# First modulation and first projections of a two-block transformer layer, worked tile by tile, on one Trainium2 core

## The reference, cut to what matters

```python
def first_block(x, c, w_in, b_gates, ..., w_ada, b_ada, ...):
    c_act = jax.nn.silu(c)
    h = layer_norm(x)
    for l in range(DEPTH):
        ada = (c_act @ w_ada[l] + b_ada[l])[:, None, :]
        sh1, sc1, g1, sh2, sc2, g2 = jnp.split(ada, 6, axis=-1)
        u = h * (1.0 + sc1) + sh1
        y = mixer(u, w_in[l], ...)      # z = u @ w_in; q/k, v, gates, attention
        ...
```

## Time and profile before

| | us |
|---|---|
| median of 3 runs | 1974.08 (1972.8 to 1978.43) |
| the profiled execution, its own time | 1963.49 |
| its span in the profile | 1961.7 |
| TensorE busy | 1897.7 |
| VectorE busy | 1419.5 |
| ScalarE busy | 1038.9 |
| mean granted clock of TensorE | 0.991 |

### The profile page before, as it was taken

The page is one execution under the profiler, slowest core; times in us unless marked ns, Lnnn a source line. Parts: engine busy times, 40 slices in busy tenths (PEclk is TensorE's granted clock), DMA queues, the critical chain, the costliest instruction groups (busy, mean ns, idle before and its releaser), DMA issues.

```text
span 1961.7 us, 37250 instructions
## 1 busy us (share of the span) xinstructions
PE 1897.7 (97%) x15702; PEld 1814.0 (92%) x15702; DVE 1419.5 (72%) x2563; ACT 1038.9 (53%) x1601; POOL 23.1 (1%) x36
## 2 busy tenths in 40 slices
PE   6999999999999999999999999999999999999998
PEld 5999999999999999999999988889999988799998
DVE  7887686687668876776675558996766589967665
ACT  3564465454446654664544434565655445666554
POOL 1100000000002000000000000000000000000000
PEclk7999999999999999999999999999999999999999
DMA  8555545548763565545465525332555443335552
GB/s 323 203 179 210 216 174 190 183 180 306 258 237 129 181 213 204 194 176 194 170 253 194 206 104 189 132 126 88 202 194 194 141 154 136 110 107 182 194 194 98
DMA packets 52770, 358.98 MB, mean 183 GB/s; under 512 B 5995, under 2 KB 8651, under 8 KB 9980
## 3 DMA queue, kind: packets, MB, share of 16 engines
q1 hardware_dynamic: 52476, 356.54, 50.8%
q10 hardware_dynamic: 128, 0.07, 0.0%
HBM read 355.41 MB, written 1.08 MB: 182 GB/s over the span
## 4 chain that ended last, share of the span: by engine, by line
PE 81%; DVE 12%; ACT 4%; issue 2%; DMA 2%; SPq 0%; ACTq 0%; DVEq 0%
PE projected L483 35%; PE projected L1534 18%; PE mixed L483 7%; PE mixed L1534 6%; PE projected L1552 2%; DVE W L2141 2%; DVE w_lo L400 2%; DVE w_lo L1476 1%; PE mixed L641 1%; PE projected L1588 1%; DMA w_mod<-in_first_ada_dram 1%; PE mixed L1686 1%; PE mixed L1659 1%; PE mixed L549 1%; PE mixed L562 1%
## 5 line engine op out<-in xcount | busy, mean ns | idle before, releaser
L400 DVE TENSOR_TENSOR w_lo<-raw,w_hi 128x1024 fp32r<-128x1024 f32 x340 | 409.2, 1226 | 211.2 <-ACT w_hi L746 210.1
L746 ACT ACTIVATE w_hi<-raw 128x1024 fp32r<-128x1024 f32 x338 | 349.3, 1056 | 291.6 <-PE projected L483 239.9
L483 PE MATMUL projected<-u_hi,w_hi 128*128 128x256 f32 x1728 | 485.3, 281 | 5.9 <-DVE w_lo L400 3.1
L483 PE MATMUL projected<-u_lo,w_hi 128*128 128x256 f32 x1728 | 479.5, 277 | 0.0
L483 PE MATMUL projected<-u_hi,w_lo 128*128 128x256 f32 x1728 | 479.3, 277 | 0.0
L483 PEld LDWEIGHTS projected<-u_hi,w_hi 128*128 128x128 f32 x1728 | 325.3, 188 | 10.6 <-issue 9.7
L483 PEld LDWEIGHTS projected<-u_hi,w_lo 128*128 128x128 f32 x1728 | 325.2, 188 | 0.0
L483 PEld LDWEIGHTS projected<-u_lo,w_hi 128*128 128x128 f32 x1728 | 325.0, 188 | 0.0
L1476 DVE TENSOR_TENSOR w_lo<-raw,w_hi 128x1024 fp32r<-128x1024 f32 x200 | 240.9, 1222 | 100.2 <-ACT w_hi L1832 100.1
L1832 ACT ACTIVATE w_hi<-raw 128x1024 fp32r<-128x1024 f32 x200 | 207.1, 1055 | 122.6 <-PE projected L1534 99.4
L1534 PE MATMUL projected<-u_hi,w_hi 128*128 128x256 f32 x960 | 267.9, 279 | 0.8 <-DVE w_lo L1476 0.8
(11 more groups left out here) (388 smaller groups left out, 3853.9 us busy)
## 6 DMA issues: line engine op xcount, KB each, us to landing
raw<-in_stream_dram SPq DMA_DIRECT2D x324, 1024.0 KB, 4.9
w_mod<-in_first_ada_dram SPq DMA_DIRECT2D x8, 1024.0 KB, 14.8
band<-bias_rows SPq DMA_DIRECT2D x1, 3072.0 KB, 13.1
x<-in_xT_dram SPq DMA_DIRECT2D x1, 1024.0 KB, 4.8
out_dram<-uf SPq DMA_DIRECT2D x4, 256.0 KB, 2.5
tri<-in_tri_dram SPq DMA_DIRECT2D x2, 384.0 KB, 4.5
c<-in_c_dram SPq DMA_DIRECT2D x1, 512.0 KB, 6.5
mask<-in_mask_dram SPq DMA_DIRECT2D x1, 384.0 KB, 25.6
```

Source lines behind the costliest of these rows:

```text
L400: eng.tensor_tensor(part(w_lo, step, half), raw_half(step, half), part(w_hi, step, half).bitcast(F32), ALU.subtract).then_inc(s_lo_dve, 1)
L483: m = pe.matmul(out, a, b, start=start and n == 0, stop=stop and n == 2, **kw)
L746: act.activation(part(w_hi, step, half), raw_half(step, half), ACT.Copy).then_inc(s_hi, 1)
```

## The change

1. **Shift on TensorE.** The first half of a `first_ada` chunk is stored the other way round (features of c on partitions), and silu(c) is also kept as a column tile `ccol` (128 x 8 x 2, each value twice). `shift(i)` is 8 matmuls in f32 with a 128 x 128 piece of the chunk as weights and 2 columns of `ccol` moving. Four banks take turns. ACT adds the bias and writes `fold` for one tile.
2. **Scale stays on DVE**, one dot product of 1024 per tile, with 1 + bias as its starting value.
3. **u by tile**: tile kt is made as soon as its scale and shift are there.
4. **TensorE follows u in three steps at once**: `shift(kt + 1)`, then for tile kt qk 0 (6 matmuls), gates (3) and from the third tile on `values(kt - 2)` of v 0 (6). These three steps (`OPENING`) are skipped in the engine's list later. The 9 idle matmuls are gone, the bias row is projected behind tile 4.
5. **DMA order**: first weight chunk before all first_ada chunks, second between the second and the third of them; the identity and bias tables behind the third.
6. **Rounding** of the second chunk (v 0) moves into the opening, between u tiles.

```diff
-        def project_first(step, x, ready, idle=0):
+        def project_first(step, x, ready):
...
-            keep_busy(pe, out, ident, idle)
...
         for step in PLAN1:
             kind, N, l, i = local(step)
+            if step in OPENING:
+                continue
...
     def sync(sp):
         sp.dma_start(x[:], A["xT"]).then_inc(s_x, 16)
         sp.dma_start(c[:], A["c"].to_broadcast([P, D])).then_inc(s_c, 16)
-        sp.dma_start(vecs[:], A["vec1"]).then_inc(s_in, 16)
-        sp.dma_start(k["ident"][:], A["ident"]).then_inc(s_in, 16)
-        sp.dma_start(onehot[:], A["onehot"]).then_inc(s_in, 16)
-        sp.dma_start(rel[0:BUCKETS, :], A["rel"]).then_inc(s_in, 16)
+        sp.dma_start(ccol[:], A["ccol"]).then_inc(s_col, 16)
+        sp.dma_start(vecs[:], A["vec1"]).then_inc(s_vec, 16)
         k["load_gates"](sp)
+        k["load_raw"](sp, 0)
         for i in range(KT):
-            if i == KT // 2:
-                k["load_raw"](sp, 0)
             sp.dma_start(w[:, i, :], A["first_ada"][i]).then_inc(s_w[i], 16)
+            if i == 1:
+                k["load_raw"](sp, 1)
+            if i == 2:
+                sp.dma_start(k["ident"][:], A["ident"]).then_inc(s_in, 16)
...
     def tensor(pe):
+        def shift(i):
+
+            pe.wait_ge(s_w[i], 16)
+            if i >= len(shifts):
+                pe.wait_ge(s_shift, i - len(shifts) + 1)
+            for kt in range(KT):
+                m = pe.matmul(shifts[i % len(shifts)][:, 0:2], w[:, i, kt * P:(kt + 1) * P], ccol[:, kt, :],
+                              start=kt == 0, stop=kt == KT - 1)
+            m.then_inc(s_shp, 1)
...
+        pe.wait_ge(s_col, 17)
+        shift(0)
+        for kt in range(KT):
+            if kt + 1 < KT:
+                shift(kt + 1)
+            if kt == 0:
+                pe.wait_ge(s_lo_dve, 2)
+                pe.wait_ge(s_gw_lo, 1)
+            if kt == 2:
+                pe.wait_ge(s_lo_dve, 4)
+            pe.wait_ge(s_u, kt + 1)
+            for half in range(2):
+                m = triple(PB[0][:, half * T:(half + 1) * T], (q_hi[:, half, kt, :], q_lo[:, half, kt, :]),
+                           (u_hi[:, kt, :], u_lo[:, kt, :]), kt == 0 and half == 0, kt == KT - 1, skip_group_check=True)
...
+            m = triple(MB[0][0:4 * MH, 0:T], (wgate_hi[:, kt, :], wgate_lo[:, kt, :]), (u_hi[:, kt, :], u_lo[:, kt, :]),
+                       kt == 0, kt == KT - 1)
...
+            if kt >= 2:
+                values(kt - 2)
+            if kt == 4:
+                pe.wait_ge(s_in, 48)
+                pe.matmul(PB[3][0:AH, :], rel[:], onehot[:], start=True, stop=True).then_inc(s_row, 1)
+        values(KT - 2)
+        pe.wait_ge(s_rowc, 1)
+        values(KT - 1).then_inc(s_used, 2)
 
     def scalar(act):
...
+        for kt in range(KT):
+            act.wait_ge(s_shp, kt + 1)
+            act.activation(fold[:, 1, kt:kt + 1], shifts[kt % len(shifts)][:, 0:1], ACT.Identity,
+                           bias=vecs[:, 0, V_ADA + kt:V_ADA + kt + 1]).then_inc(s_shift, 1)
+            act.wait_ge(s_shift, kt + 1)
+            act.wait_ge(s_uf, kt + 1)
+            act.activation(u_hi[:, kt, :], sq[:, kt, :], ACT.Identity, bias=fold[:, 1, kt:kt + 1]).then_inc(s_uh, 1)
+            if kt < 2:
+                k["round_first"](act, 1, kt)
...
     def vector(dve):
+        def scale(i):
+
+            dve.wait_ge(s_w[i], 16)
+            part = w[:, i, HALF:2 * HALF]
+            dve.tensor_tensor_reduce(out=part, in0=part, in1=k["cact"][:], scale=1.0, scalar=plus[:, i:i + 1],
+                                     op0=ALU.mult, op1=ALU.add, accum_out=fold[:, 0, i:i + 1]).then_inc(s_scale, 1)
...
+        scale(0)
...
+        for half in range(2):
+            k["rest_first"](dve, 0, half)
         dve.wait_ge(s_rstd, 1)
+        for kt in range(KT):
+            if kt:
+                scale(kt)
+            dve.wait_ge(s_scale, kt + 1)
+            dve.scalar_tensor_tensor(out=sq[:, kt, :], in0=cen[:, kt, :], scalar=fold[:, 0, kt:kt + 1], in1=rstd[:],
+                                     op0=ALU.mult, op1=ALU.mult).then_inc(s_uf, 1)
+            if kt in (1, 2):
+                k["rest_first"](dve, 1, kt - 1)
+            if 1 <= kt < KT - 1:
+                rest_of_u(kt - 1)
+            if kt >= KT - 2:
+                rest_of_u(kt)
```

More of the change, by code:

```diff
@@ L428, in load_gates, with round_first, rest_first @@
         sp.dma_start(bgate[:], A["bgate"]).then_inc(s_small, 16)
[L430 to L438, removed]
+    def round_first(act, c, half):
+        act.wait_ge(s_landed[c], 16)
+        act.activation(part(w_hi, MAIN1[c], half), raw_half(MAIN1[c], half), ACT.Copy).then_inc(s_hi, 1)
+    def rest_first(dve, c, half):
+        subtract(dve, MAIN1[c], half)
     k["sems"] = {"s_hi": s_hi, "s_lo_dve": s_lo_dve, "s_used": s_used, "s_u": s_u, "s_uf": s_uf, "s_uh": s_uh,
@@ L451, in sync @@
     def sync(sp):
-        for c in range(1, len(CHUNKS1)):
+        for c in range(2, len(CHUNKS1)):
             if c == RING:
@@ L753, in scalar @@
             if kind == "u":
-                for kt in range(KT):
+                for kt in range(KT) if N else ():
                     act.wait_ge(s_uf, 8 * N + kt + 1)
@@ L958, in vector @@
             if kind == "u":
-                for kt in range(KT + 1):
+                for kt in range(KT + 1) if N else ():
                     if kt < KT:
@@ new lines, in tensor, with triple, values @@
+    def tensor(pe):
+        def triple(out, a, b, start, stop, **kw):
+            passes = [(a[0], b[0]), (a[0], b[1]), (a[1], b[0])]
+            for n, (one, other) in enumerate(passes):
+                m = pe.matmul(out, one, other, start=start and n == 0, stop=stop and n == 2, **kw)
+            return m
+        def shift(i):
[6 more added lines that the diff above has]
+            m.then_inc(s_shp, 1)
+        def values(kt):
+            for tt in range(TT):
+                t = slice(tt * P, (tt + 1) * P)
+                m = triple(PB[1][:, tt * T:(tt + 1) * T], (u_hi[:, kt, t], u_lo[:, kt, t]),
+                           (v_hi[:, kt], v_lo[:, kt]), kt == 0 and tt == 0, kt == KT - 1, skip_group_check=True)
+            return m
+        q_hi, q_lo = (a[:, 0, :].rearrange("p (h k n) -> p h k n", h=2, k=KT) for a in (w_hi, w_lo))
+        v_hi, v_lo = (a[:, 1, :].rearrange("p (h k n) -> p k h n", h=2, k=KT) for a in (w_hi, w_lo))
@@ L2380, in vector @@
+        dve.wait_ge(s_dve, 1)
+        k["dve_steps"][0] = 1
         dve.wait_ge(s_c, 17)
[L2381 to L2393, removed]
@@ new lines, in vector @@
+        dve.wait_ge(s_gw_hi, 1)
+        dve.tensor_tensor(wgate_lo[:], wgate[:, 0], wgate_hi[:].bitcast(F32), ALU.subtract).then_inc(s_gw_lo, 1)
+        for half in range(2):
+            k["rest_first"](dve, 0, half)
+        dve.wait_ge(s_rstd, 1)
+        for kt in range(KT):
[10 more added lines that the diff above has]
+                rest_of_u(kt)
@@ L2565, in layout @@
         "xT": a["x"][0].T.reshape(KT, P, T).transpose(1, 0, 2),
[L2566 removed]
+        "c": a["c"], "ccol": np.repeat(a["c"].reshape(KT, P).T[:, :, None], 2, axis=2),
         "ident": np.eye(P, dtype=np.float32),
         "mask": mask_table(), "dist": distance_table(),
[L2569 removed]
+        "first_ada": np.concatenate([columns(a["w_ada"][:1, :, 0:D], P)[0], tiled_rows(a["w_ada"][0, :, D:2 * D])], axis=2),
         "stream1": in_order(chunks, CHUNKS1, COUNT1),
```

69 lines of the change are left out of this document (41 added, 28 removed).

## The result

The changed kernel takes **1990.41 us** (median of 10 runs, 1983.97 to 1998.32); the kernel before takes 1977.63 us (10 runs beside them, 1972.8 to 1985.84). The ratio is 1.0064, 95% interval 1.0043 to 1.0085: 0.6% slower, by about 12.8 us. The forecast was 1977.6 us, no difference that can be told; what came is rival B, the clock that stays at 1.2 GHz through the opening, at nearly its full length. The median lies 0.4 us above the range.

The account below looks back on a forecast made before the run. TensorE, busy 1897.7 of 1961.7 us, was taken to bound the kernel: -2.8 us from the earlier v 1 and +6.3 from the low clock gave +3.5, so 1977.6 us from a median of 1974.1; range 1968 to 1990.

Parts of the forecast that it names:

- rival B: Opening: clock stays at 1.2 GHz throughout, +6 to +15 us, 1989 at full length; chance 0.20.
- Landings and u 0: Start of opening: first_ada 0 lands at 14.0, 2 at 21.5, 7 at 34.2; first u tile at 21.8 us.
- Price of a shift, 1.68 us, and TensorE as the bound: Opening: 16 instructions of 0.105 us a shift; TensorE needs 3.4 us a tile, above landing 2.49 and DVE 2.1.
- rival C: Opening: a shift is much cheaper than 0.105 us an instruction, landings and DVE bound, 1968 us; chance 0.07.
- The sum at 2.4 GHz: Opening: qk 1 can start at 47.3, v 1 starts at 55.9 after a 2.9 us wait; 2.8 us gained.
- The clock term: Opening: clock falls at about 18 us, is back at 32, then one more fall of 3.3 us; costs 6.3 us.
- the rows at 192.4 and 152.9: Earlier trace, two-column matmuls: clock fell for 3.3 us after a mixed stretch; without pause ahead it stayed at 1.00.
- bounds of 1 and 18: Opening, cost of low clock: 1 us if back with tile 1 (about 25), 18 if never before the tail (about 60).
- Behind that both kernels have the same order, and the gain stays: After v 1 starts: the opening's gain of 2.8 us is kept to the end.
- Rival D: Behind the opening: waits just move, DVE's chain from the end of qk 0 counts; forecast gives it 3.1 of 5.9 us.
- The median: Whole kernel: forecast goes by the timed runs' median, 1974.1 us, 10.6 above the profiled execution, giving 1977.6.

Follow-up runs that it names:

- e3: Changed kernel with every shift's 8 matmuls done twice; 2013.89 us (one timing).
- e1: Changed kernel with each shift matmul's moving operand widened from 2 to 128 columns by a zero stride; 1978.15 us, ratio 1.001 to the kernel before.
- e2: Changed kernel with twelve idle matmuls filling TensorE's pause between shift 1 and u 0; 1982.85 us, ratio 1.0015 to the kernel before.
- e6: e5 with ten idle matmuls between shift 1 and u 0; 1975.4 us, ratio 1.0005 to the kernel before.
- e9: e1 with 13 idle matmuls (2.90 us) on TensorE ahead of qk 1; 1985.49 us (one timing).
- e10: e6 with 13 idle matmuls (2.90 us) on TensorE ahead of qk 1; 1983.75 us (one timing).
- e8: The kernel before, unchanged, profiled once more; 1967.23 us (one timing).
- e11: e6 with the gate_rows step one chunk later in the list; 1974.71 us, ratio 0.9982 to the kernel before.
- e5: e1 with w_lo of v 1 ahead of the convolution of qk 0 on DVE; 1978.49 us, ratio 1.001 to the kernel before.
- e7: Changed kernel with shift back on DVE, each chunk holding its tile's shift and scale, and e5's order; 1977.65 us, ratio 1.0008 to the kernel before.
- e12: e7 with the gate_rows step one chunk later in the list; 1970.78 us, ratio 0.9976 to the kernel before.

## Why the prediction failed

- **Landings and u 0: right.** DVE waited for first_ada chunks to 14.50 and 23.10, and u_lo of tile 0 ended at 22.16; with the mean matmul 1.15 later than before these are 13.4, 22.0 and 21.0, forecast 14.0, 21.5 and 21.8.
- **Price of a shift, 1.68 us, and TensorE as the bound: right** (16.80, 58.26, e3). At 1.00 every shift shows it, 1.70 us from one start to the next; rival C falls. The Trainium skill, "TensorE: Matmul & The Clock Gate", section "Back-to-back issue gap", gives its 25 ns for an isolated matmul; with new weights for each instruction this trace does not agree. e1 adds that 2 and 128 columns cost the same.
- **The sum at 2.4 GHz: right.** It gave v 1 at 55.9. e1 with its one fall of 3.4 us (1.7 more, and a start 0.6 later) should have it at 58.2; it has it at 58.4, with 2.6 us of wait for w_lo where 2.9 were forecast.
- **The clock term, "back after about 10 us, at 32, and one more fall: 6.3 us": wrong.** This is the step that failed: the mechanism was right, its length was not. The clock fell at 20.9 and came back at 58.4, where 18 and 32 were forecast. Measured against e1, which has 3.4 us of it, the narrow shifts cost 14.3 us at v 1; with the 1.7 of e1's own fall the term is 16.0, not 6.3. I held the rows at 192.4 and 152.9 to be one for and one against, and took a middle value between bounds of 1 and 18 that no row narrowed. But the alternation that fell at 192.4 was one burst; here it came eight times in a row, and no row showed the clock coming back in such a mix. (I also passed over a return: the earlier trace rows show one at 38.7, after 4.7 us of wide matmuls, and one at 195.7, after 3.3 us at the low clock. In e1 and e2 it first came back after 3.4.) Rival B gave the outcome and its price rightly (+15; 13.5 came). Its chance should have been the larger one. The Trainium skill, "TensorE: Matmul & The Clock Gate", section "HAM oscillation — how this bites in real kernels", spoke for B by bursts parted by waits for data. It named the outcome, but not the way that it came here: from 22.30 to 58.4 TensorE waited for nothing, and in e2 the clock fell with TensorE busy throughout.
- **"Behind that both kernels have the same order, and the gain stays": wrong**, though it cost the forecast nothing here, since a lateness stays (13.5 at v 1, 13.2 at the gate column). An earliness doesn't: e6 brings 3.9 us to v 1 and 0.8 to the gate column, and in e9 and e10 2.9 us of delay vanish. Rival D was right about half of this, the waits for DVE (1.5 us); the other half is a fall of the clock behind v 1 (1.7 us) that nobody forecast. With the clock back after 3.4 us (e1) the gate column is 0.3 us before the old kernel's, not 2.8, and no difference in the median can be told.
- **The median**: forecast from 1974.1, where ten runs give 1977.6. These 3.5 us are by themselves more than the 0.4 by which the range was missed.

## What to carry to other kernels

Before a small matrix-vector product goes to TensorE, ask at which clock it and everything around it will run: a trace that shows the engine 96% busy can still stand at half the clock. If such products stand between wide ones, give them a wide moving operand (a stride of zero does it) and look at the granted clock again; here that was worth some 11 to 12 us and made a shift no longer. And before an opening is shortened, delay it on purpose: if a few us of idle matmuls vanish downstream, see first where they go: into waits, then the next engine's order (here DVE's) has to be changed, or into a stretch at the low clock.

## What the runs showed that was not expected

- Behind two-column f32 matmuls the granted clock fell to 0.50 with TensorE busy all the time (e2). With such matmuls and wide ones in turn it stayed there for 37.5 us, of which 1.4 idle (changed kernel).
- The time of a 16-instruction shift was the same with 2 and with 128 moving columns: 1.84 to 1.95 us at 1.00, 3.19 to 3.41 at 0.50. Its length is not set by these columns, and about doubles at half the clock.
- Wide matmuls in the second block run at one of two paces, and the pace changes from profile to profile. The chain of waits near 1400 us, kernel before and then changed kernel:

```profile
1403.66 10.88 PE projected L1534 x96
1414.54 5.44 PE mixed L1534 x48
```

```profile
1405.06 11.31 PE projected L1530 x96
1416.38 5.65 PE mixed L1530 x48
```

That is 113.3 ns a matmul against 117.8, at a granted clock of 1.00 in both. The kernel before, e6, e8 and e11 have the first pace here, the changed kernel, e1 to e5, e7, e9, e10 and e12 the second. Since e6 has it one way and e10, e6 with a delay, the other, it isn't the change's doing. The spans with the first pace are 1959.7 to 1966.7 us, those with the second 1970.8 and more; e6 and e10 are 15.2 apart, though their gate columns are not. At 4.5 ns for each of the 3936 matmuls of these two forms in the second block, if the pace held for all, it would be 18 us (an estimate). So it likely makes most of the gap between the profiled run of the kernel before (1963.49) and its median, and of what the span grew beyond 12.8 us. What sets the pace was not tried and stays open.
